# Fetching expert rows of both tables in one gather, from one shared pool of row buffers

## The reference, cut to what matters

```
def peer_ffn(x, w_pq, sub_keys, u_emb, v_emb):          # x: (rows, 1024)
    ...                                                # eid: 8 x 16 expert ids for each row, gate: their softmax
    act = gelu(einsum('chkd,cd->chk', u_emb[eid], xc))
    return einsum('chk,chkd->cd', gate * act, v_emb[eid])
```

## Time and profile before

| | |
|---|---|
| median of 3 runs | 1099.0 us (1096.78 to 1109.1) |
| span of the profiled execution | 1099.1 us |
| busy | PE 783.8, DVE 756.8, POOL 660.6, ACT 410.7 us |
| moved by DMA | 381.92 MB, 304.81 of them by the queue of GpSimd's gathers |

### The profile page before, as it was taken

The page is one execution under the profiler, slowest core; times in us unless marked ns, Lnnn a source line. Parts: engine busy times, 40 slices in busy tenths (PEclk is TensorE's granted clock), DMA queues, the critical chain, the costliest instruction groups (busy, mean ns, idle before and its releaser), DMA issues.

```text
span 1099.1 us, 13767 instructions
## 1 busy us (share of the span) xinstructions
PE 783.8 (71%) x4093; PEld 382.7 (35%) x4093; DVE 756.8 (69%) x1924; ACT 410.7 (37%) x1155; POOL 660.6 (60%) x584
## 2 busy tenths in 40 slices
PE   7898997553977759878647676766775675646867
PEld 3565674110534436535313233332322432211111
DVE  1341295999575654599997599999653588998442
ACT  1234122333544553233325264553574332334221
POOL 0000036778688676477677666467488477778773
PEclk9999998767888898978877889788587788876999
DMA  9904569999999999999999999999899999999995
GB/s 354 300 21 184 209 211 388 366 378 368 315 353 331 341 377 410 379 411 383 337 364 381 389 392 376 361 366 397 327 390 410 411 412 410 409 382 331 388 380 205
DMA packets 121660, 381.92 MB, mean 347 GB/s; under 512 B 15722, under 2 KB 40122, under 8 KB 116082
## 3 DMA queue, kind: packets, MB, share of 16 engines
q0 software_dynamic: 83696, 304.81, 73.4%
q1 hardware_dynamic: 37890, 76.23, 19.2%
HBM read 378.29 MB, written 4.40 MB: 348 GB/s over the span
## 4 chain that ended last, share of the span: by engine, by line
DVE 40%; PE 24%; POOL 16%; DMA 11%; issue 7%; ACT 3%; SPq 0%; ACTq 0%; DVEq 0%
PE bank L437 18%; DVE rows L1267 9%; POOL rows L1723 8%; PE acc L437 5%; DMA rows<-in_peer_u,eid 4%; POOL rows L1741 4%; DVE ql_t L1530 4%; DVE small L1529 4%; DMA rows<-in_peer_v,eid 3%; DVE shared L1561 2%; DVE shared L1572 2%; DVE more_u L1267 2%; DMA x<-in_peer_u,eid 2%; DVE first_u L1267 2%; PE bank L440 1%
## 5 line engine op out<-in xcount | busy, mean ns | idle before, releaser
L437 PE MATMUL acc<-rows,spread 128*64 128x512 f32 (+1 forms) x1152 | 364.9, 717 | 128.5 <-DMA rows<-in_peer_v,eid 117.0
L1723 POOL DMA_INDIRECT rows<-in_peer_v,eid x288 | 336.1, 1167 | 180.7 <-PE acc L437 89.8
L1267 DVE CUSTOM_DVE_ANT_0 rows<-rows,xr 128x1024 f32<-128x1024 f32 x184 | 221.3, 1222 | 98.4 <-DMA rows<-in_peer_u,eid 96.9
L1741 POOL DMA_INDIRECT rows<-in_peer_u,eid x184 | 204.4, 1111 | 68.7 <-issue 53.4
L437 PEld LDWEIGHTS acc<-rows,spread 128*64 128x64 f32 (+1 forms) x1152 | 95.1, 157 | 349.6 <-issue 303.3
L1741 POOL DMA_INDIRECT first_u<-in_peer_u,eid x37 | 42.9, 1160 | 109.5 <-DVE eid L1622 98.1
L958 ACT ACTIVATE gelus<-dots 128x2 f32<-128x2 f32 x144 | 28.9, 201 | 190.3 <-DVE dots L1267 189.9
L967 ACT ACTIVATE spread<-wide_consts,wts 128x64 f32<-128x64 f32 (+1 forms) x288 | 83.7, 337 | 5.9 <-PE acc L437 1.2
L960 ACT ACTIVATE wts<-gelus,gate 128x1 f32<-128x1 f32 x288 | 69.1, 287 | 4.7
L440 PE MATMUL bank<-ident,shared 128*128 128x128 f32 (+4 forms) x162 | 31.0, 312 | 52.8 <-DVE shared L1292 15.0
L1267 DVE CUSTOM_DVE_ANT_0 more_u<-more_u,xr 128x1024 f32<-128x1024 f32 x37 | 45.4, 1226 | 19.2 <-DMA more_u<-in_peer_u,eid 18.9
(11 more groups left out here) (242 smaller groups left out, 1205.7 us busy)
## 6 DMA issues: line engine op xcount, KB each, us to landing
wring<-in_w_pq SPq DMA_DIRECT2D x12, 1024.0 KB, 8.4
rows<-in_w_pq SPq DMA_DIRECT2D x3, 2048.0 KB, 8.9
z<-in_w_pq SPq DMA_DIRECT2D x5, 1024.0 KB, 8.2
wring<-in_cache_ckv SPq DMA_DIRECT2D x40, 128.0 KB, 7.5
rows<-in_peer_v,eid POOLq DMA_INDIRECT x288, 8.2
rows<-in_w_in SPq DMA_DIRECT2D x2, 2048.0 KB, 15.9
rows<-in_w_out SPq DMA_DIRECT2D x2, 2048.0 KB, 7.5
wring<-in_w_out SPq DMA_DIRECT2D x4, 1024.0 KB, 12.8
```

The source lines that it names most:

```text
L437: return T.matmul(o, lhsT=l, rhs=r, start=start, stop=stop, skip_group_check=True)
L1267: V.tensor_tensor_reduce(out=u, in0=u, in1=xr[:, j, :], scale=1.0, scalar=0.0, op0=ALU.mult, op1=ALU.add, accum_out=dots[:, k:k + 1]).then ...
L1723: nc.gpsimd.indirect_dma_start(out=v_ring[n % RV], out_offset=None, in_=inp["peer_v"], in_offset=bass.IndirectOffsetOnAxis(ap=eid[t][:, n ...
L1741: nc.gpsimd.indirect_dma_start(out=u_ring[U_PLACE[n]], out_offset=None, in_=inp["peer_u"], in_offset=bass.IndirectOffsetOnAxis(ap=eid[t][: ...
```

## The change

- Of the slots from 24 on, every fourth (n % 4 == 3; 66 in all) is TOGETHER: one gather brings rows of 8 KB from a new table `peer_uv`, made on the host, where an expert's u and v rows stand side by side. It lands in two adjacent buffers, c and c+1. It stands where u(n) stood; v(n) is not fetched again five slots later. GpSimd issues 510 gathers instead of 576.
- The two rings become one pool of CELLS = 15 buffers of the tensor `rows`, with the same two guests for u alone. The number of buffers is the same.
- `give_cells` fixes at build time which cell each fetch gets: the one that a table says is emptied first, where a u cell counts as emptied 4.5 slots after its fetch's slot and a v cell 13 slots after its slot. A TOGETHER fetch takes the adjacent pair whose later one is emptied first. A fetch waits for the cell's last user, which may be a dot or a sum.
- The opening waits of the weight buffers move with the cells (OPENS).

```diff
-RU, RV, RD = 7, 8, 4
+CELLS, RD = 15, 4
...
+TOGETHER = [n >= 24 and n % 4 == 3 for n in range(sum(SLOTS))]
+OPENS = [(2.5, ("pq", 1, 0))] * 4 + [(6.5, ("pq", 2, 0))] * 4 + [(11.5, ("pq", 3, 0))] * 4 + [(8.5, ("z", 3, 1))] + [(-1, None)] * 2
...
+def give_cells():
+    emptied = [at for at, w in OPENS] + [a for a, b in U_GUESTS]
+    held = [("opens", w) for at, w in OPENS] + [(None, None)] * len(U_GUESTS)
+    uses = [0] * len(held)
+    def take_cell(c, kind, n):
+        before, held[c], emptied[c] = held[c], (kind, n), n + (4.5 if kind == "u" else 13)
+        return before
+    for n in range(sum(SLOTS) + V_LAG):
+        if n < sum(SLOTS) and TOGETHER[n]:
+            c = min(range(CELLS - 1), key=lambda c: (max(emptied[c:c + 2]), -min(emptied[c:c + 2])))
...
+            U_AFTER[n], V_AFTER[n] = take_cell(c, "u", n), take_cell(c + 1, "v", n)
+        elif n < sum(SLOTS):
+            c = min([*range(CELLS), *(CELLS + i for i, (a, b) in enumerate(U_GUESTS) if a <= n <= b)], key=lambda c: emptied[c])
...
+        m = n - V_LAG
+        if m >= 0 and not TOGETHER[m]:
+            c = min(range(CELLS), key=lambda c: emptied[c])
...
             def fetch_v(n):
-                if n >= RV:
-                    pool.wait_ge(sums_done, (n - RV) // PAIR + 1)
...
+                if not TOGETHER[n]:
+                    emptied(V_AFTER[n])
+                    fetch(n, "peer_v", cells[V_CELL[n]], V_COUNT[n])
...
-                    if U_LAST[n] >= 0:
-                        pool.wait_ge(dots_done, U_LAST[n] + 1)
+                    emptied(U_AFTER[n])
+                    if TOGETHER[n]:
+                        emptied(V_AFTER[n])
+                        fetch(n, "peer_uv", rows[:, U_CELL[n]:U_CELL[n] + 2, :].rearrange("p a b -> p (a b)"), U_COUNT[n])
+                    else:
+                        fetch(n, "peer_u", cells[U_CELL[n]], U_COUNT[n])
```

More of the change, by code:

```diff
@@ L77 @@
 U_GUESTS = [(24, 118), (144, sum(SLOTS) - 1)]
[L78 to L84, removed]
+TOGETHER = [n >= 24 and n % 4 == 3 for n in range(sum(SLOTS))]
+OPENS = [(2.5, ("pq", 1, 0))] * 4 + [(6.5, ("pq", 2, 0))] * 4 + [(11.5, ("pq", 3, 0))] * 4 + [(8.5, ("z", 3, 1))] + [(-1, None)] * 2
+U_CELL, U_COUNT, U_AFTER, V_CELL, V_COUNT, V_AFTER = ({} for i in range(6))
+def give_cells():
[8 more added lines that the diff above has]
+            c = min(range(CELLS - 1), key=lambda c: (max(emptied[c:c + 2]), -min(emptied[c:c + 2])))
+            uses[c] += 1
+            U_CELL[n], V_CELL[n], U_COUNT[n], V_COUNT[n] = c, c + 1, (c, uses[c]), (c, uses[c])
+            U_AFTER[n], V_AFTER[n] = take_cell(c, "u", n), take_cell(c + 1, "v", n)
+        elif n < sum(SLOTS):
+            c = min([*range(CELLS), *(CELLS + i for i, (a, b) in enumerate(U_GUESTS) if a <= n <= b)], key=lambda c: emptied[c])
+            uses[c] += 1
+            U_CELL[n], U_COUNT[n], U_AFTER[n] = c, (c, uses[c]), take_cell(c, "u", n)
+        m = n - V_LAG
+        if m >= 0 and not TOGETHER[m]:
+            c = min(range(CELLS), key=lambda c: emptied[c])
+            uses[c] += 1
+            V_CELL[m], V_COUNT[m], V_AFTER[m] = c, (c, uses[c]), take_cell(c, "v", m)
+give_cells()
 FIRST_SLOT = [0, EARLY, 128, 256]
@@ L137, in build @@
         page_sb = small[0:1, 128:128 + NB * NPG].bitcast(I32)
-        rows = sb("rows", [128, 13, DM])
+        rows = sb("rows", [128, CELLS, DM])
         rows_f = rows[:, :, :].rearrange("p a b -> p (a b)")
-        u_ring = [first_u[:, :], more_u[:, :]] + [rows[:, i, :] for i in range(5)] + [b[:, :] for b in x_b]
-        v_ring = [rows[:, i, :] for i in (5, 6, 7, 12, 8, 9, 10, 11)]
+        cells = [rows[:, i, :] for i in range(CELLS)] + [b[:, :] for b in x_b]
         spread = [sb(f"spread{i}", [128, PAIR, WIDE]) for i in range(RD)]
@@ L383, in lodged @@
             return lodge_view(lodge[i], w, c)
-        u_in = [sem(f"u{i}_in") for i in range(RU + 2)]
-        v_in = [sem(f"v{i}_in") for i in range(RV)]
+        cell_in = [sem(f"cell{i}_in") for i in range(CELLS + 2)]
         dots_done = sem("dots_done")
@@ L1264, in dot_slot @@
                 k, j = n % RC, n % PAIR if t < 2 else 0
-                u = u_ring[U_PLACE[n]]
-                dve.wait_ge(u_in[U_PLACE[n]], (U_USE[n] + 1) * 16)
+                u, (c, count) = cells[U_CELL[n]], U_COUNT[n]
+                dve.wait_ge(cell_in[c], 16 * count)
                 V.tensor_tensor_reduce(out=u, in0=u, in1=xr[:, j, :], scale=1.0, scalar=0.0,
@@ L1715, in _, with emptied, fetch @@
                                 ).then_inc(bias_in, 16)
-            def fetch_v(n):
-                t = [k for k in tiles if n >= BASE[k]][-1]
-                if n in (0, 3, 4):
-                    ready(pool, {0: ("pq", 2, 0), 3: ("z", 3, 1), 4: ("pq", 3, 0)}[n])
-                if n >= RV:
-                    pool.wait_ge(sums_done, (n - RV) // PAIR + 1)
[L1723 to L1726, removed]
+            def emptied(before):
+                kind, m = before
+                if kind == "opens" and m:
+                    ready(pool, m)
+                elif kind == "u":
+                    pool.wait_ge(dots_done, m + 1)
+                elif kind == "v":
+                    pool.wait_ge(sums_done, m // PAIR + 1)
+            def fetch(n, table, o, count):
+                t = [k for k in tiles if n >= BASE[k]][-1]
+                nc.gpsimd.indirect_dma_start(
+                    out=o, out_offset=None, in_=inp[table],
+                    in_offset=bass.IndirectOffsetOnAxis(ap=eid[t][:, n - BASE[t]:n - BASE[t] + 1], axis=0)
+                ).then_inc(cell_in[count[0]], 16)
+            def fetch_v(n):
+                if not TOGETHER[n]:
+                    emptied(V_AFTER[n])
+                    fetch(n, "peer_v", cells[V_CELL[n]], V_COUNT[n])
             for t in tiles:
@@ L2008, in laid_out @@
     pool = a["cache_k"].shape[1]
+    a["peer_uv"] = np.concatenate([a["peer_u"], a["peer_v"]], 2)
     a["cache_ckv"] = a["cache_ckv"][0]
@@ L2018 @@
           "rel_bias", "g_attn", "w_in", "g_q", "w_uq", "g_kv", "w_uk", "w_uv", "w_out", "g_ffn", "w_pq", "peer_keys",
-          "peer_u", "peer_v", "g_final"]
+          "peer_u", "peer_v", "peer_uv", "g_final"]
 OUTPUTS = {"y_p": (SEQ, DM), "y_s": (32, DM), "ckv_p": (SEQ, KVL), "kr_p": (SEQ, ROPE), "k_p": (SEQ, 128),
@@ L2038 @@
         inp[name] = nc.dram_tensor(f"in_{name}", a.shape, mybir.dt.from_np(a.dtype), kind="ExternalInput").ap()
-    inp["peer_u"], inp["peer_v"] = (inp[n].rearrange("l e d -> (l e) d") for n in ("peer_u", "peer_v"))
+    for n in ("peer_u", "peer_v", "peer_uv"):
+        inp[n] = inp[n].rearrange("l e d -> (l e) d")
     for name, a in shape_constants().items():
```

13 lines of the change are left out of this document (3 added, 10 removed).

## The result

| | before | after |
|---|---|---|
| median | 1104.05 us (4 runs, 1096.78 to 1113.3) | 1110.26 us (4 runs, 1106.74 to 1112.15) |
| ratio | 1 | 1.0098, interval 1.0063 to 1.0132 |
| span of the profiled execution | 1099.1 us | 1110.3 us |
| GpSimd busy | 660.6 us | 573.7 us |

A forecast was written before the change was run, and what follows sets the result against it. The limit was taken to change hands: GpSimd's issuing (middle and last stage), DMA at 410 GB/s, VectorE's own work. Terms -13 - 4 - 3 + 4 + 7 = -9 us took 1099 to 1090 us, range 1072 to 1114.

The forecast's parts named there:

- point 4: Opening: early u and v rows can be issued sooner, so VectorE waits less; -3 us, bounds -9 and 0.
- point 1: Middle stage, slots 48 to 84: 9 gathers fewer save GpSimd's issue time; -13 us, bounds -20 and -4.
- point 5: Cells in place of rings: five fetches in slots 128 to 255 wait for sum n-12; +4 us, bounds 0 and +14.
- points 3, 6: 3: last stage, fewer gathers up to the DMA ceiling, -4 us; 6: slot 255 waits for dot 252, delaying later gathers, +7.
- The reasoning on the ceiling: Middle stage: at a DMA ceiling of 410 GB/s instead of 335, 111.3 us could become 91, a gain of 20.
- Point 2: One 8 KB gather costs GpSimd 0.94 us, upper bound twice that; no change taken for the bytes themselves.
- the rival of two for one: Rival: an 8 KB gather costs GpSimd as much as two; +6 us, 1105 us, chance 0.13.
- Rival "cells run short": Rival: u rows wait for sum n-12 while TensorE trails VectorE; +17 us, 1116 us, chance 0.20.
- Its middle term of -5: Middle stage under the rival of short cells: a gain of only 5 us.

The follow-up runs named there:

- mt_nt3: Changed kernel with pairs fetched together only in slots 40 to 99 and from 252 on, 36 pairs, none tight: 1092.46 us, ratio 0.9936 to the kernel before.
- no_tight_two: Changed kernel's plan cut to 38 pairs without tight waits, each pair fetched by two gathers of 4 KB rows: 1108.91 us, ratio 1.0088 to the kernel before.
- no_tight: Changed kernel, TOGETHER only where both cells' last users are dot n-5 or sum n-13 or earlier, 38 pairs: 1094.8 us, ratio 0.9961 to the kernel before.
- no_tight_again: Changed kernel with only the 38 pairs without tight waits, run once more on the third chip: 1096.66 us, ratio 0.9966 to the kernel before.
- before_wait252_again: The kernel before with one wait more, u(255) waits for dot 252, repeated on the third chip: 1111.57 us, ratio 1.0114 to the kernel before.
- apart255_again: Changed kernel with slot 255 fetched apart, repeated on the second chip: 1107.27 us, ratio 1.0064 to the kernel before.
- before_six: The kernel before with each u(n) from slot 32 on also waiting for dot n-6: 1107.42 us, ratio 1.0068 to the kernel before.
- after_again: The changed kernel once more, unaltered, on the second chip: 1109.29 us, ratio 1.0077 to the kernel before.
- apart255: Changed kernel with slot 255 fetched apart, on the slower first chip: 1115.69 us, ratio 0.982 to the kernel before on that chip.

## Why the prediction was wrong, step by step

The range (1072 to 1114) holds 1110; the sign is wrong. By stage, in us, forecast and shown (after, means as above):

```
                     forecast                        shown
opening              -3  (point 4)                   -3.8
36 to 84             -13 (point 1)                   -1.9
84 to 252            +4  (point 5)                   +7.4
252 to 287           -4 +7 = +3 (points 3, 6)        +6.9
```

1. **Point 1 is the step that failed: 11 of the 17.6 us.** The sum counted 9 saved gathers at their full price, because GpSimd hardly waited in this stage before. But the changed plan puts eight tight waits (for dot n-4, sum n-12 or n-11) of five pairs into this very stage, and some at dot n-5. The three longest stalls there stand in front of pairs (slots 47, 75, 83; the first is not even a tight one, it waits for dot n-5):

```profile
290.07 1.68 POOL L1751 DMA_INDIRECT rows<-in_peer_uv,eid  x1 [6.17 <-DVE dots L1289]
...
369.96 0.94 POOL L1751 DMA_INDIRECT rows<-in_peer_uv,eid  x1 [6.26 <-PE acc L459]
...
396.82 0.94 POOL L1751 DMA_INDIRECT rows<-in_peer_uv,eid  x1 [6.81 <-PE acc L459]
```

  19 us of standing still, against the 13 us of busy time saved. I had priced the tighter waits in slots 128 to 255 only and named TensorE's sums as the cover that may end, without looking which slots of the middle stage wait for them (75 for sum 63; 83 for sum 72, n-11, the only one so near). VectorE's waits didn't fall, and 26.7 us of them are now for the pairs' own rows, which are issued after the stalls. The reasoning on the ceiling was right, as mt_nt3 shows with 387 GB/s and -11.6 us, with no tight pair. It has waits too in that stage (26.6 us of GpSimd), so that their sum alone doesn't tell a good plan from a bad one; it has 18 pairs there to pay them with, where after has 12. So it is shown that 12 pairs of this plan give 1.9 us and not 13; that the three stalls took the rest is argued from their place and length, not shown by a run.

2. *Point 2 was right.* 1.16 us, one packet for each row; the rival of two for one falls, by this row and by no_tight_two. A dot holds such a gather as it holds the others: in the timeline above a dot ends at 1000.04 and the pair's gather, begun in it, at 1000.85. The prediction put this as a rule, and the trace has it for most: in before, 177 of the 216 gathers that start inside a dot take over 0.99 us, and 37 of the 360 others; in after, 25 of the 33 pair gathers that start inside a dot. The Trainium skill (DMA: Bandwidth & Descriptors, SWDGE vs HWDGE vs iDMA) puts a packet at 4096 bytes "preferably"; the packet records here have 8192.

3. *Point 3: the rate came, the gain did not.* The last stage runs at 413 GB/s in place of 388, as forecast. But the slots from 252 on take 86.8 and 87.0 us in no_tight and no_tight_again, 87.1 in no_tight_two and 87.3 in mt_nt3, where 86.0 was before: fetching together earns nothing there, in any plan. The window of dots 252 to 287 in no_tight_again says why:

```profile
988.00:1075.00 87.00, 61.65 (x130) 14.01 (x131) 48.28 (x84) 24.43 (x90) 64.29 (x62) 0.86 1.01 395
```

  87.0 x 395 = 34.4 MB against 31.7: whatever the rate gains is spent on rows that were already there before. I reckoned with a rate and left out the stock.

4. *Point 4* gave -3.8 for -3, in part by luck. VectorE's wait before dot 9 did shrink, from 6.1 us to 3.2 and 1.3 in the two traces of after. But no_tight_two, which fetches the pairs of slots 27, 31 and 35 apart, has 108.7 us from dot 0 to 36 and not 105.3, against 110.2 before: most of the gain seems to come from the first pairs and not from the waits that I had looked at.

5. *Points 5 and 6 had the mechanism and too small a price.* Slots 84 to 252 cost 7.4 us (forecast 4), nearly all of it from 128 on, where GpSimd stalls for 126 us and I had reckoned five late fetches. I had VectorE wait there for u rows; its waits for them halved and those for TensorE's banks doubled. For slot 255 the delay came as reckoned: u(261) goes out at 1013.11, 15.4 us after the start of dot 252, where it was 4.8, so 10.6 us later for 10.5. What it costs I had put at 7 us net; before_wait252_again prices it at 7.3 us by its trace from 252 to 287 and 12.5 us by its ratio (7.5 to 17.6). The stretch alone is thus what I forecast, and the whole run costs rather more; up to slot 252 that trace is 2.7 us behind before's (1.8 of them at dot 0 already) although the kernels don't differ there.

6. *Rival "cells run short"* (1116 us, 0.20) is the case that came, in a milder form. It isn't TensorE's lag alone, dots hold GpSimd for 145.8 us and sums for 75.5. Its middle term of -5 was nearer than the forecast's -13.

7. *Which wait was the tight one?* By apart255_again, not the one. Taking that of dot n-3 away gives 2.0 us, not clear of noise; taking away every wait nearer than dot n-5 or sum n-13 (25 of them), and 28 pairs with them, gives 14.5. Where one stall is removed the next wait takes part of it over, as the two stalls of 3.2 us in apart255_again show. But a tight wait isn't the whole price: before_six has no wait nearer than dot n-6 and loses 0.7%, no_tight_two has no tight one and loses 0.9%.

What stays open: on the first chip apart255 beat before by 1.8% and on the second it lost by 0.6%. No run tells why. No run has 38 pairs chosen without regard to tightness, so that the worth of the condition by itself isn't known. And the runs put 0.32 us on a saved gather of 1.44 us only as an average over the plan of no_tight; which of the 38 earned it was not tried.

## What to carry to other kernels

A prefetch queue has two prices, the time to issue and the rows that it is ahead. Before an issue is saved by holding a buffer longer, write out for each fetch whose release it waits for, and price the tightest ones as stalls of everything behind them, in the very stage that is to gain. Merge only where both buffers come free in good time (here: the last user 5 dots or 13 sums back), and only in stages where issuing is the limit: the two together turned +0.8% into -0.6%. The last stage is a warning: by the prediction's reading issuing was the limit there too, and merging earned nothing, in any plan.

## What the hardware showed that I had not expected

- A gather of 128 rows costs GpSimd the same whether its rows have 4 or 8 KB: shortest 932 ns in both, medians 938 and 939 ns.

```profile
L1751 POOL DMA_INDIRECT rows<-in_peer_v,eid x222: 932/939/1992, 155.7 to 1082.8; - x111
...
L1751 POOL DMA_INDIRECT rows<-in_peer_uv,eid x66: 932/938/1987, 222.9 to 1077.7; - x66
```

- By the page a row of 8 KB seems to land as soon as one of 4 KB, though I had added 1.3 us (issue to landing, median us, by destination and source):

```profile
rows<-in_peer_v,eid POOLq DMA_INDIRECT x222, 8.4
rows<-in_peer_u,eid POOLq DMA_INDIRECT x183, 8.3
rows<-in_peer_uv,eid POOLq DMA_INDIRECT x66, 8.3
```

  That median mixes two cases. A gather right after a stall finds little in flight (in the window over the hole above the DMA share is 0.43) and lands early. Over five traces (after, after_again, no_tight, no_tight_again, mt_nt3) the pair gathers whose landing the trace has (127 of 244) take 7.3 us after a stall (45) and 9.5 us without one (82), where the gathers just before and behind these take 8.3. So a row of 8 KB lands some 0.7 to 1.1 us later under the same load, not far from what I had added.

- One wait of one instruction, 15.5 us long, in a kernel of 1100 us, costs 1.1%. In after the like stall (12.4 us) lies under a VectorE that is busy 14.77 of 15.4 us, and VectorE hardly waits for it at the time. But 15.4 us at 168 GB/s in place of before's 352 are 2.8 MB not fetched, which is 7 us at 413 GB/s (an estimate from these rates), and the stage behind, which already runs at 413, has no room to make them up.
